# Where the squares in front of the up projection and of the embedding gate are added: GpSimd in place of VectorE and TensorE

## The chip, the cores and the metric

The kernel runs on one core of one Trainium2 chip. The metric is the device time of one execution in microseconds (us), the median of several runs. The engines are TensorE (PE in the rows; PEld is its weight load), VectorE (DVE), ScalarE (ACT), GpSimd (POOL) and SyncE (SP), which issues DMAs.

## The reference, cut to what matters

One step of a two-layer decoder over 512 prompt tokens and 8 sample tokens, together T = 520 tokens of D = 1024 features. Layer 0 mixes tokens with an mLSTM, layer 1 with sliding-window attention. Around the mixer every layer does the same:

```python
h = h + rmsnorm(mixer(rmsnorm(h, g_pre_mix)), g_post_mix)
h = h + rmsnorm(conv_ffn(rmsnorm(h, g_pre_ffn)), g_post_ffn)   # d_ff = 2816, causal conv of width 3
h = h + sigmoid(rmsnorm(h, g_ple) @ w_gate) * (p[i] @ w_proj)  # per-layer embedding
# rmsnorm(x, g) = x * rsqrt(mean(x * x) + eps) * g
```

The case is about two of these norms: the one in front of the ConvFFN (`g_pre_ffn`, stage `up`) and the one in front of the embedding gate (`g_ple`, stage `ple`). Each needs the sum of h squared over the 1024 features of every token.

## The kernel before, in words

Activations lie feature-major: 128 features on the partitions, KT = 8 tiles of features, the 520 tokens along the free dimension, in two halves q = 0 and q = 1 of HT = 260 tokens. Every weight tile and every activation tile is split into a high and a low part (`wH`, `wL`, `xH`, `xL`), and a product is three matmuls (`product`, `half_product`, L1173 to L1189): high by high, low by high, high by low. ScalarE makes the high parts, VectorE the low parts (`low`, L1827; `x_low`, L1851). Weight chunks come in by DMA into a ring of slots, issued by SyncE in the order of the stages. All order is written out by hand: each engine has its own program, and engines wait for each other on counting semaphores.

Around the change a layer goes like this, once after the mixer (stages `mout` or `sout`, then `up`) and once after the down projection (`down`, `pw`, then `ple`):

- PE ends the product y for half 0, then for half 1. VectorE sums the squares of y into `acc` (`add_unit`, L1897), PE sums `acc` over the partitions with a matmul by ones (`y_sum`, L1240), ScalarE takes the root (`root`, L763), VectorE the reciprocal (`one_over`, L1835).
- VectorE then runs through the `residual` steps (L1858), eight tiles k for each half q: y times gain times 1/rms into `cv` (L1865), h plus that (L1870), and the low part of the next input (L1853). All three read two operands from SBUF. ScalarE follows tile by tile with `inputs` (L780): the high part `xH`, and the square of h into `square(stage, q, k)`, a 128x260 tile.
- PE starts the next stage on half 0 alone (`first_half`, L1482, three chunks), then catches up on half 1 as its tiles come (`second_half`, L1494), then takes whole chunks (`chunk`, L1194). A chunk may start once the PSUM bank that it takes has been read (`free_after`, L1207): whole chunk 3 needs the read of chunk 0, chunk 5 that of chunk 3.
- The sum over the features of the squares is made in between. For q = 0 of `up` VectorE folds the eight tiles into one (`fold_squares`, L1843), and PE sums it over the partitions by one 128x128 matmul with ones (`square_sum`, L1231). For the three others of a layer (`GROUPED`, L108: `up` q = 1, `ple` q = 0, `ple` q = 1) PE adds: `square_group` (L1220) sends four tiles at a time through four 32-column groups of the array, ScalarE copies the result back (`group_sums`, L775), and `square_sum` makes the total of it. ScalarE takes the root (`pre_root`, L769) and VectorE the reciprocal (`pre_one_over`, L1839), by which the PSUM reads of the stage scale (`first_read`, `second_read`, `scaled_read`).

GpSimd works early (stretch before 190 us), and at the start of layer 1; in the stretches around the change it has only a small memset, and DMAs to issue.

Of the kernel before, what the change touches and what calls it, by code (L numbers as in the profile page):

```python
# [8 lines left out]
ALU = mybir.AluOpType  # L9
ACT = mybir.ActivationFunctionType  # L10
# [4 lines left out]
D = 1024  # L15
KT = D // P
SEQ, DEC = 512, 8
T = SEQ + DEC
HT = T // 2
# [85 lines left out]
ROOT = {("kv", 0): 1, ("mout", 0): 2, ("mout", 1): 3, ("down0", 0): 4, ("down0", 1): 5, ("qkv", 0): 6,  # L105
        ("sout", 0): 7, ("sout", 1): 8, ("down1", 0): 9, ("down1", 1): 10}
PREROOT = {(s, q): 2 * i + q + 1 for i, s in enumerate(("up0", "ple0", "up1", "ple1")) for q in range(2)}
GROUPED = {sq: n + 1 for n, sq in enumerate(sq for sq in PREROOT if sq[0][:2] != "up" or sq[1])}  # L108
POST = {"up0": "mout", "ple0": "down0", "up1": "sout", "ple1": "down1"}
G_PRE_MIX, G_POST_MIX, G_PRE_FFN, G_POST_FFN, G_PLE = range(5)  # L110

# [26 lines left out]
def build(nc, g):  # L138
    with ExitStack() as ctx:
# [19 lines left out]
        def sem(name):  # L159
            return ctx.enter_context(nc.semaphore(name))  # L160
# [26 lines left out]
        sq = sb("sq", [P, 2, T])  # L187
# [142 lines left out]
                                                          sem("gate_weights_ready"), sem("gate_parts_read"),  # L330
                                                          sem("gate_rows"), sem("gate_rows_read"))
        s_part, s_sqadd = sem("gate_parts_done"), sem("squares_added")
        s_psum, s_psumr = sem("pre_squares_by_group"), sem("pre_squares_by_group_read")
        s_fold = sem("pre_squares_added")
        s_raw0 = [sem(f"first_weights_in{c}") for c in range(2)]
        s_high0, s_low0 = sem("first_weights_high"), sem("first_weights_low")
        s_mm, s_read = sem("chunk_done"), sem("tile_read")
# [86 lines left out]
        def square(stage, q, k):  # L424

            if stage[:2] == "up":
                return squares_up[int(stage[2])][:, KT * q + k, :]
            if q == 0 and k < KT // 2:
                return sg[k // 2][:, tokens(k % 2)]
            return squares_ple[:, KT * q + k - KT // 2, :]  # L430
# [190 lines left out]
        def _(pool):  # L621
# [78 lines left out]
            pool.wait_ge(s_out, 16 * stored)  # L700
            pool.wait_ge(s_cps, 16)

            for layer in range(NL):
                up, down, ple = f"up{layer}", f"down{layer}", f"ple{layer}"

                if layer:
                    pool.wait_ge(s_hid, FT)
                    pool.wait_ge(s_out, 16 * stored)
                    pool.dma_start(convw[:], g.convw[layer]).then_inc(s_cw, 16)
                    pool.dma_start(prev[:], g.conv_prev[layer]).then_inc(s_cw, 16)  # L710

                pool.wait_ge(s_afin if layer == 0 else s_rope, NH + 1 if layer == 0 else 2 + KT)
                nc.gpsimd.memset(u[:, :, 0:2], 0.0).then_inc(s_pad, 1)
                if layer == 0:
                    for i, (r0, r1) in enumerate(COPIES):
                        pool.wait_ge(s_mm, CHUNK0["up0"] + 4 * i + 4)
                        pool.dma_start(g.v_s[r0:r1], g.vc_in[r0 + 1:r1 + 1]).then_inc(s_out, 16)
                    pool.wait_ge(s_mm, CHUNK0["up0"] + 4 * len(COPIES) + 4)
                    pool.dma_start(g.conv_old, g.conv_prev[:, :, :, 1, :]).then_inc(s_out, 16)
                    stored += len(COPIES) + 1  # L720
                pool.wait_ge(s_hid, FT * (layer + 1))
                pool.dma_start(g.newrows[layer], newrows[:]).then_inc(s_out, 16)
                stored += 1

                pool.dma_start(pin[:], g.p[layer]).then_inc(s_p, 16)
                if layer == 0:
                    pool.wait_ge(s_mm, CHUNK0["ple0"] + 1 + NEXTRA)
                    nc.gpsimd.memset(qpad[:], 0.0).then_inc(s_qz, 1)
                    for dst, src in ((sinks[:], g.sinks), (cos_t[:], g.cos_t), (sin_t[:], g.sin_t)):
                        pool.dma_start(dst, src).then_inc(s_swc, 16)  # L730
                    band_and_sinks(pool)
                    pool.wait_ge(s_qp, 1)
                    pool.dma_start(g.k_p, qk[:, 0:2, SEQ - WINDOW:SEQ]).then_inc(s_out, 16)
                    pool.dma_start(g.v_p, vs[:, :, SEQ - WINDOW:SEQ]).then_inc(s_out, 16)
                    pool.dma_start(g.k_s, kc[:, :, :, 1:WINDOW + 1]).then_inc(s_out, 16)
                    pool.wait_ge(s_vtr, 3)
                    pool.dma_start(g.v_s[WINDOW - 1], vnew[:]).then_inc(s_out, 16)
                    last_rotation(pool)
                    pool.wait_ge(s_ss, SUM["qkv", 0])
                    nc.gpsimd.memset(acc[:], 0.0).then_inc(s_acc, 1)  # L740
                    pool.wait_ge(s_rope, 2 + KT)
                    nc.gpsimd.memset(spad, 0.0).then_inc(s_spz, 1)
                    stored += 4
                    assert stored == STORED_L0
# [3 lines left out]
        def _(act):  # L748
# [20 lines left out]
            def pre_root(stage, q):  # L769

                act.wait_ge(s_squ, KT + PREROOT[stage, q])
                nc.scalar.activation(rstd[:, tokens(q)], sums[:, q, 0:HT], ACT.Sqrt, bias=eps[:, 0:1],
                                     scale=1.0 / (32 * D if (stage, q) in GROUPED else D)).then_inc(s_rootp, 1)

            def group_sums(stage, q):  # L775

                act.wait_ge(s_psum, GROUPED[stage, q])
                nc.scalar.activation(square(stage, q, 0), sums[:, q, 0:HT], ACT.Copy).then_inc(s_psumr, 1)

            def inputs(stage, k, q, layer, norm):  # L780

# [134 lines left out]
            def feed_forward(layer, mixer, y, beside):  # L916
# [33 lines left out]
                for k in range(KT):  # L950
                    inputs(up, k, 1, layer, G_PRE_FFN)
                    if k == 2:
                        high(up, 3)
                group_sums(up, 1)
                pre_root(up, 1)
                high(up, 4)
                high(up, 5)
# [68 lines left out]
                p_copy(5)  # L1026
                high(ple, 1)
                ple_input(0, 1)
                group_sums(ple, 0)
                p_copy(6)  # L1030
                high(ple, 2)
                ple_input(1, 1)
# [4 lines left out]
                for k in range(4, KT):  # L1037
                    ple_input(k, 1)
                high(ple, 3)
                group_sums(ple, 1)  # L1040
                high(ple, 4)
                pre_root(ple, 1)
                for c in range(5, KT):
# [128 lines left out]
        def _(pe):  # L1172
# [44 lines left out]
                elif r + k0 >= 2:  # L1217
                    pe.wait_ge(s_read, r + k0 - 1)

            def square_group(stage, q, part):  # L1220

                pe.wait_ge(s_sq, SQ0[stage] + KT * q + 4 * part + 4)
                if part == 0:
                    pe.wait_ge(s_root, ROOT[POST[stage], q])
                for j in range(4):
                    mm = nc.tensor.matmul(sums[32 * j:32 * j + 32, q, 0:HT], ones[:, 0:32], square(stage, q, 4 * part + j),  # L1226
                                          start=(part == 0), stop=(part == 1), skip_group_check=True)
                if part:
                    mm.then_inc(s_psum, 1)

            def square_sum(stage, q):  # L1231

                if (stage, q) in GROUPED:
                    pe.wait_ge(s_psumr, GROUPED[stage, q])
                else:
                    pe.wait_ge(s_root, ROOT[POST[stage], q])
                    pe.wait_ge(s_fold, int(stage[2]) + 1)
                nc.tensor.matmul(sums[:, q, 0:HT], ones, square(stage, q, 0), start=True, stop=True).then_inc(s_squ, 1)

            def y_sum(stage, q):  # L1240
# [272 lines left out]
            def feed_forward(layer, mixer, beside):  # L1513
# [15 lines left out]
                for k in range(4):  # L1529
                    for c in range(SPLIT):  # L1530
                        second_half(up, c, k, k + 1)
                square_group(up, 1, 0)
                square_group(up, 1, 1)
                for c in range(2):
                    second_half(up, c, 4, 5)
                square_sum(up, 1)
# [41 lines left out]
                for j in range(KT):  # L1578
                    c, jj = CHUNK0[pw] + j // 4, j % 4
                    if jj == 0:  # L1580
                        weights_ready(c)
                    for q in range(2):
                        if j >= 2:
                            pe.wait_ge(s_pwr, 2 * KT * layer + 2 * (j - 2) + q + 1)
                        for k in range(EKT):
                            mm = half_product(c, EKT * jj + k, (pH, pL), k, q, p_bank(j)[:, q, 0:HT], k == 0, k == EKT - 1)
                        mm.then_inc(s_mm if jj == 3 and q == 1 else s_pw, 1)
                    if j == 0:
                        y_sum(down, 1)
                    if j == 5:  # L1590
                        square_group(ple, 0, 0)
                        square_group(ple, 0, 1)

                yd = YREAD0[down]
                square_sum(ple, 0)
# [3 lines left out]
                for k in range(3):  # L1599
                    for c in range(SPLIT):  # L1600
                        second_half(ple, c, k, k + 1)
                square_group(ple, 1, 0)
                square_group(ple, 1, 1)
                for c in range(SPLIT):
                    second_half(ple, c, 3, 4)
                square_sum(ple, 1)
# [217 lines left out]
        def _(dve):  # L1824
# [14 lines left out]
            def pre_one_over(stage, q):  # L1839
                dve.wait_ge(s_rootp, PREROOT[stage, q])  # L1840
                chain.link(nc.vector.reciprocal(rstd[:, tokens(q)], rstd[:, tokens(q)]))

            def fold_squares(stage, q):  # L1843

                dve.wait_ge(s_sq, SQ0[stage] + KT * q + KT)
                tiles = squares_up[int(stage[2])][:, KT * q:KT * q + KT, :]
                for n in (4, 2):
                    chain.link(nc.vector.tensor_tensor(tiles[:, 0:n, :], tiles[:, 0:n, :], tiles[:, n:2 * n, :], ALU.add))
                nc.vector.tensor_tensor(tiles[:, 0, :], tiles[:, 0, :], tiles[:, 1, :], ALU.add).then_inc(s_fold, 1)

            def x_low(stage, k, q, layer, norm):  # L1851
                dve.wait_ge(s_xh, XSET[stage] + KT * q + k + 1)
# [347 lines left out]
            def feed_forward(layer, mixer, y, beside):  # L2200
# [35 lines left out]
                low(up, 2)  # L2236
                add_unit(mixer, 5, 1)
                add_unit(mixer, 6, 1)
                fold_squares(up, 0)

                dve.wait_ge(s_pad, layer + 1)
                one_over(mixer, 1, cg[:, tokens(1)])
# [524 lines left out]
```

## Time and profile before

| | |
|---|---|
| Median of 3 runs | 1296.57 us (1296.37 to 1296.8) |
| Span of the profiled execution | 1294.8 us, granted TensorE clock 1.000 |
| Busy: PE, DVE, ACT, POOL | 1287.4, 891.1, 594.0, 75.0 us |
| `square_group`, L1226 | 96 records of PE, 380 to 408 ns each, four at a time |
| VectorE's fold, L1848 and L1849 | 6 instructions |
| `group_sums`, L778 | 6 copies of ScalarE |

Only the span of the profiled execution is given, not its time as the runs count it; the median of the runs lies 1.8 us above the span. Times in the rows are from the span's start. A start is when an engine took the instruction up; an instruction that is blocked after that shows a longer duration. Instructions of VectorE and ScalarE overlap by some 0.08 us, so that starts, not durations, give the pace. The ends of PE's records are modelled, and there too the starts give the pace.

### The profile page before, as it was taken

Reading aid. Unit: us, or ns where it says so; the run is one execution under the profiler, and the core shown is the slowest. Engines: PE = TensorE matmul, PEld = TensorE weight load, DVE = VectorE, ACT = ScalarE, POOL = GpSimd, SP = SyncE. Lnnn points to the kernel's source line nnn. Section 1 sums busy time; section 2 is a strip of 40 time slices with the busy share of each in tenths; the row PEclk is TensorE's granted clock in tenths of the full one; section 3 lists DMA queues with packets and bytes.
Section 4 is the critical chain, followed back from the end, with each engine's and each line's share of the span. In section 5 each row is a group of like instructions: output and inputs, shape, how many; then the busy total and the mean of one; then the engine's idle time right before and its main releaser. Section 6 shows DMA issues by size and latency. Waiting matters only on the chain.

```text
span 1294.8 us, 25277 instructions
## 1 busy us (share of the span) xinstructions
PE 1287.4 (99%) x10786; PEld 1254.7 (97%) x10786; DVE 891.1 (69%) x1602; ACT 594.0 (46%) x1060; POOL 75.0 (6%) x117
## 2 busy tenths in 40 slices
PE   9999999999999999999999999999999999999998
PEld 8999989999999999999999978999999999999998
DVE  7899776987777774223897787688777777422385
ACT  6214565544444443223855677554444444222381
POOL 1112230000100000000031020000000000000000
PEclk9999999999999999999999999999999999999999
DMA  5435521213343233222314232311322323322231
GB/s 199 155 100 194 198 99 53 103 58 106 95 105 94 87 111 114 90 90 78 138 59 148 68 97 81 113 52 50 98 94 87 98 84 110 114 90 90 79 130 67
DMA packets 35616, 131.84 MB, mean 102 GB/s; under 512 B 4516, under 2 KB 5260, under 8 KB 35184
## 3 DMA queue, kind: packets, MB, share of 16 engines
q1 hardware_dynamic: 29664, 111.33, 26.8%
q0 software_dynamic: 5408, 18.26, 4.3%
q8 instruction: 85, 1.39, 0.4%
q10 hardware_dynamic: 432, 0.64, 0.2%
q14 instruction: 27, 0.22, 0.1%
HBM read 121.26 MB, written 10.08 MB: 101 GB/s over the span
## 4 chain that ended last, share of the span: by engine, by line
PE 95%; DVE 3%; ACT 1%; DMA 0%; issue 0%; ACTq 0%; DVEq 0%
PE tile L1177 24%; PE tile L1181 24%; PE tile L1179 24%; PE tile L1187 5%; PE tile L1188 5%; PE tile L1189 4%; PE tile L1649 1%; PE side L1187 1%; PE side L1188 1%; PE side L1189 1%; PE sums L1226 0%; DMA raw<-in_w_kv 0%; PE sums L1700 0%; PE sums L1348 0%; PE sums L1707 0%
## 5 line engine op out<-in xcount | busy, mean ns | idle before, releaser
L756 ACT ACTIVATE wH<-raw 128x1024 fp32r<-128x1024 f32 (+1 forms) x190 | 210.9, 1113 | 377.4 <-DMA raw<-in_w_up 145.9
L1177 PE MATMUL tile<-xH,wH 128*128 128x260 f32 x1798 | 362.7, 283 | 0.1
L1181 PE MATMUL tile<-xH,wL 128*128 128x260 f32 x1798 | 362.4, 283 | 0.0
L1179 PE MATMUL tile<-xL,wH 128*128 128x260 f32 x1798 | 361.8, 283 | 0.0
L1832 DVE TENSOR_TENSOR wL<-raw,wH 128x1024 fp32r<-128x1024 f32 (+1 forms) x190 | 245.7, 1294 | 154.5 <-ACT wH L756 150.4
L1177 PEld LDWEIGHTS tile<-xH,wH 128*128 128x128 f32 x1798 | 277.1, 188 | 3.5 <-issue 3.0
L1181 PEld LDWEIGHTS tile<-xH,wL 128*128 128x128 f32 x1798 | 277.2, 188 | 0.0
L1179 PEld LDWEIGHTS tile<-xL,wH 128*128 128x128 f32 x1798 | 276.4, 188 | 0.0
L1880 DVE SCALAR_TENSOR_TENSOR u<-tile,rstd 128x520 f32<-128x520 f32 x96 | 67.2, 700 | 119.5 <-PE tile L1181 119.4
L1177 PE MATMUL tile<-hidH,wH 128*128 128x260 f32 x616 | 124.3, 283 | 0.0
L1181 PE MATMUL tile<-hidH,wL 128*128 128x260 f32 x616 | 123.8, 282 | 0.0
L1179 PE MATMUL tile<-hidL,wH 128*128 128x260 f32 x616 | 123.8, 282 | 0.0
L1187 PE MATMUL tile<-xH,wH 128*128 128x260 f32 x400 | 116.0, 290 | 0.1
L1188 PE MATMUL tile<-xL,wH 128*128 128x260 f32 x400 | 113.1, 283 | 0.0
L1189 PE MATMUL tile<-xH,wL 128*128 128x260 f32 x400 | 112.8, 282 | 0.0
L1179 PEld LDWEIGHTS tile<-hidL,wH 128*128 128x128 f32 x616 | 95.1, 188 | 0.0
L1181 PEld LDWEIGHTS tile<-hidH,wL 128*128 128x128 f32 x616 | 94.9, 188 | 0.0
L1177 PEld LDWEIGHTS tile<-hidH,wH 128*128 128x128 f32 x616 | 94.8, 188 | 0.0
L1187 PEld LDWEIGHTS tile<-xH,wH 128*128 128x128 f32 x400 | 75.3, 188 | 2.8 <-issue 2.3
L1188 PEld LDWEIGHTS tile<-xL,wH 128*128 128x128 f32 x400 | 75.3, 188 | 0.3
L1189 PEld LDWEIGHTS tile<-xH,wL 128*128 128x128 f32 x400 | 75.3, 188 | 0.0
L977 ACT ACTIVATE cv<-u,taps 128x520 f32<-128x520 f32 x44 | 36.2, 824 | 48.2 <-DVE u L1880 47.8
(446 smaller groups left out, 1913.9 us busy)
## 6 DMA issues: line engine op xcount, KB each, us to landing
raw<-in_w_up SPq DMA_DIRECT2D x88, 512.0 KB, 3.6
raw<-in_w_down SPq DMA_DIRECT2D x32, 704.0 KB, 4.1
raw<-in_w_ple SPq DMA_DIRECT2D x16, 512.0 KB, 5.6
raw<-in_w_qo SPq DMA_DIRECT2D x12, 512.0 KB, 3.6
raw<-in_w_qkv SPq DMA_DIRECT2D x12, 512.0 KB, 3.5
raw<-in_w_kv SPq DMA_DIRECT2D x10, 512.0 KB, 3.7
cring<-in_c_in POOLq DMA_DIRECT2D x8, 512.0 KB, 4.8
out_c_s<-cring POOLq DMA_DIRECT2D x8, 512.0 KB, 3.2
```

The costliest lines, as they stand in the source:

```text
L756: nc.scalar.activation(wH[j][:, 0:n], raw[j][:, 0:n], ACT.Copy).then_inc(s_high, 1)
L977: nc.scalar.activation(dst[:], u[:, r, 2:], ACT.Identity, bias=taps[:, r, 3:4], scale=taps[:, r, 2:3]).then_inc(s_ca, 1)
L1177: nc.tensor.matmul(out[:, q, 0:HT], wh, x[0][:, k, tokens(q)], start=first, stop=False)
L1179: nc.tensor.matmul(out[:, q, 0:HT], wh, x[1][:, k, tokens(q)], start=False, stop=False)
L1181: mm = nc.tensor.matmul(out[:, q, 0:HT], wl, x[0][:, k, tokens(q)], start=False, stop=last)
L1187: nc.tensor.matmul(out, wh, x[0][:, k, tokens(q)], start=first, stop=False)
L1188: nc.tensor.matmul(out, wh, x[1][:, k, tokens(q)], start=False, stop=False)
L1189: return nc.tensor.matmul(out, wl, x[0][:, k, tokens(q)], start=False, stop=last)
L1649: nc.tensor.matmul(banks[half][:, e, at0 + 2 * HD - HD * m + k0:at0 + 3 * HD], queries[r, gp, m * P:m * P + P], qk[r, gp // 2, k0:HD * m + ...
L1832: nc.vector.tensor_tensor(wL[j][:, 0:n], raw[j][:, 0:n], wH[j][:, 0:n].bitcast(F32), ALU.subtract).then_inc(s_low, 1)
L1880: nc.vector.scalar_tensor_tensor(out=halves(dst), in0=bank(stage, c)[0:rows, :, 0:HT], scalar=scale, in1=halves(rstd[0:rows, :]), op0=ALU. ...
```

## The change

GpSimd gets a `fold_squares` of its own, and runs it four times in a layer: for `up` q = 0 and q = 1 behind the memset of `u`, and for `ple` q = 0 and q = 1 behind the load of `pin`. Each is a chain of seven adds of 128x260 tiles in place, total += square k for k = 1 to 7; an add waits for its square and for the add before it. VectorE's fold, PE's `square_group` and ScalarE's `group_sums` go. `square_sum` waits for GpSimd's last add, and stands where it stood.

```diff
-GROUPED = {sq: n + 1 for n, sq in enumerate(sq for sq in PREROOT if sq[0][:2] != "up" or sq[1])}
+FOLDED = {sq: n + 1 for n, sq in enumerate(PREROOT)}
...
+            folds = Chain(pool, s_folds)
+
+            def fold_squares(stage, q):
+
+                total = square(stage, q, 0)
+                pool.wait_ge(s_sq, SQ0[stage] + KT * q + 2)
+                for k in range(1, KT):
+                    if k > 1:
+                        pool.wait_ge(s_sq, SQ0[stage] + KT * q + k + 1)
+                    step = nc.gpsimd.tensor_tensor(total, total, square(stage, q, k), ALU.add)
+                    if k < KT - 1:
+                        folds.link(step)
+                step.then_inc(s_pooled, 1)
...
                 nc.gpsimd.memset(u[:, :, 0:2], 0.0).then_inc(s_pad, 1)
+                for q in range(2):
+                    fold_squares(up, q)
...
                 pool.dma_start(pin[:], g.p[layer]).then_inc(s_p, 16)
+                for q in range(2):
+                    fold_squares(ple, q)
...
-                                     scale=1.0 / (32 * D if (stage, q) in GROUPED else D)).then_inc(s_rootp, 1)
-
-            def group_sums(stage, q):
-
-                act.wait_ge(s_psum, GROUPED[stage, q])
-                nc.scalar.activation(square(stage, q, 0), sums[:, q, 0:HT], ACT.Copy).then_inc(s_psumr, 1)
+                                     scale=1.0 / D).then_inc(s_rootp, 1)
...
-                if (stage, q) in GROUPED:
-                    pe.wait_ge(s_psumr, GROUPED[stage, q])
-                else:
-                    pe.wait_ge(s_root, ROOT[POST[stage], q])
-                    pe.wait_ge(s_fold, int(stage[2]) + 1)
+                pe.wait_ge(s_root, ROOT[POST[stage], q])
+                pe.wait_ge(s_pooled, FOLDED[stage, q])
...
-                square_group(up, 1, 0)
-                square_group(up, 1, 1)
                 for c in range(2):
                     second_half(up, c, 4, 5)
                 square_sum(up, 1)
...
-                    if j == 5:
-                        square_group(ple, 0, 0)
-                        square_group(ple, 0, 1)
...
-                square_group(ple, 1, 0)
-                square_group(ple, 1, 1)
                 for c in range(SPLIT):
                     second_half(ple, c, 3, 4)
                 square_sum(ple, 1)
...
-                fold_squares(up, 0)
```

The order of GpSimd's instructions at the start of layer 0's `up`, before:

```order
L618 TENSOR_TENSOR xL<-kvq,xH 128x520 x2
L713 MEMSET u 128x2x2
L717 DMA out_v_s<-in_vc_in 16x4096 x3
L717 DMA out_v_s<-in_vc_in 16x3968
L719 DMA out_conv_old<-in_conv_prev 11264x8
L722 DMA out_newrows<-newrows 128x440
L725 DMA pin<-in_p 128x1040
```

and in the change, up to the next instruction that was there before:

```order
L617 TENSOR_TENSOR xL<-kvq,xH 128x520 x2
L726 MEMSET u 128x2x2
L711 TENSOR_TENSOR squares_up_101<-squares_up_101 128x260 x14
L732 DMA out_v_s<-in_vc_in 16x4096 x3
L732 DMA out_v_s<-in_vc_in 16x3968
L734 DMA out_conv_old<-in_conv_prev 11264x8
L737 DMA out_newrows<-newrows 128x440
L740 DMA pin<-in_p 128x1040
L711 TENSOR_TENSOR u<-u 128x260 x3
L711 TENSOR_TENSOR u<-u,squares_ple 128x260 x4
L711 TENSOR_TENSOR squares_ple<-squares_ple 128x260 x7
L745 MEMSET qpad 128x656
```

Fourteen adds come in ahead of the copies of the value cache (`out_v_s`), and fourteen between the load of `pin` and the memset of `qpad`; layer 1 has the same, with nothing behind its last fourteen.

The order of PE's instructions around the sum for `up` q = 1, layer 0, before (`tile` and `side` are PSUM banks, `wH_52` and the like the ring's slots):

```order
L1189 MATMUL side<-xH,wL_59 128x260
L1226 MATMUL sums<-squares_up_101,const 32x260 [waits root_ready,squared]
L1226 MATMUL sums<-squares_up_101,const 32x260 x3
L1226 MATMUL sums<-squares_up_101,const 32x260 [waits squared]
L1226 MATMUL sums<-squares_up_101,const 32x260 x3
L1187 MATMUL tile<-xH,wH_52 128x260 [waits x_ready]
L1188 MATMUL tile<-xL,wH_52 128x260
L1189 MATMUL tile<-xH,wL_53 128x260
L1187 MATMUL tile<-xH,wH_55 128x260
L1188 MATMUL tile<-xL,wH_55 128x260
L1189 MATMUL tile<-xH,wL_56 128x260
L1238 MATMUL sums<-squares_up_101,const 128x260 [waits pre_squares_by_group_read]
```

and in the change:

```order
L1198 MATMUL side<-xH,wL_59 128x260
L1196 MATMUL tile<-xH,wH_52 128x260 [waits x_ready]
L1197 MATMUL tile<-xL,wH_52 128x260
L1198 MATMUL tile<-xH,wL_53 128x260
L1196 MATMUL tile<-xH,wH_55 128x260
L1197 MATMUL tile<-xL,wH_55 128x260
L1198 MATMUL tile<-xH,wL_56 128x260
L1233 MATMUL sums<-squares_up_101,const 128x260 [waits pre_squares_added_by_pool,root_ready]
```

The eight matmuls by 32 columns are gone, and the one by 128 columns waits for GpSimd in place of ScalarE's copy.

## Rows read from the trace of the kernel before

**Rows 1.** The page's first part: busy us (share of the span) xinstructions.

```profile
PE 1287.4 (99%) x10786; PEld 1254.7 (97%) x10786; DVE 891.1 (69%) x1602; ACT 594.0 (46%) x1060; POOL 75.0 (6%) x117
```

**Rows 2.** Chain that ended last, layer 1's `up`: start us, us, engine, tile, line.

```profile
846.84 1.79 DVE cg L1837
...
875.75 0.61 DVE u L1880
876.41 0.51 PE tile L1177 x2
```

**Rows 3.** Timeline of PE, layer 0's `up`: start us, us, engine, instruction, count.

```profile
231.20 0.60 PE L1249 MATMUL sums<-acc,const 128*128 128x260 f32 x2
...
261.98 0.40 PE L1181 MATMUL tile<-xH,wL 128*128 128x260 f32 x2
262.42 0.50 PE L1177 MATMUL tile<-xH,wH 128*128 128x260 f32 x2
```

**Rows 4.** Timeline of DVE, the same stretch; in brackets idle before, and its releaser.

```profile
218.35 0.49 DVE L1853 SCALAR_TENSOR_TENSOR xL<-h,front,xH 128x260 fp32r<-128x260 f32 x1 [1.10 <-ACT xH L783]
...
228.19 0.96 DVE L1901 TENSOR_TENSOR acc<-acc,sq 128x260 f32<-128x260 f32 x2
...
232.85 1.78 DVE L1837 RECIPROCAL cg<-cg 128x260 f32<-128x260 f32 x1 [1.36 <-ACT cg L766]
...
244.25 1.77 DVE L1841 RECIPROCAL rstd<-rstd 128x260 f32<-128x260 f32 x1
...
261.67 0.69 DVE L1880 SCALAR_TENSOR_TENSOR u<-tile,rstd 128x520 f32<-128x520 f32 x1
```

**Rows 5.** Timeline of PE, layer 0's `ple`, around the group for q = 1.

```profile
640.64 0.28 PE L1188 MATMUL side<-xL,wH 128*128 128x260 f32 x1
640.76 0.28 PE L1189 MATMUL side<-xH,wL 128*128 128x260 f32 x1
640.97 1.08 PE L1226 MATMUL sums<-squares_ple,const 128*32 128x260 f32 x16
...
643.17 0.60 PE L1238 MATMUL sums<-squares_ple,const 128*128 128x260 f32 x2
...
647.91 0.41 PE L1177 MATMUL tile<-xH,wH 128*128 128x260 f32 x2
```

**Rows 6.** Timeline of DVE, layer 0's `ple`.

```profile
617.22 0.49 DVE L1853 SCALAR_TENSOR_TENSOR xL<-h,front,xH 128x260 fp32r<-128x260 f32 x1 [0.51 <-ACT xH L783]
...
618.85 0.49 DVE L1853 SCALAR_TENSOR_TENSOR xL<-h,front,xH 128x260 fp32r<-128x260 f32 x1 [0.40 <-ACT xH L783]
...
623.24 0.49 DVE L1853 SCALAR_TENSOR_TENSOR xL<-h,front,xH 128x260 fp32r<-128x260 f32 x1 [0.75 <-ACT xH L783]
...
638.40 1.77 DVE L1841 RECIPROCAL rstd<-rstd 128x260 f32<-128x260 f32 x1
...
644.32 1.78 DVE L1841 RECIPROCAL rstd<-rstd 128x260 f32<-128x260 f32 x1 [2.22 <-ACT rstd L772]
646.13 0.43 DVE L1893 TENSOR_TENSOR u<-tile,rstd 128x260 f32<-128x260 f32 x1
```

**Rows 7.** View of one line: duration ns min/median/max, first and last start us, forms.

```profile
L611 POOL TENSOR_TENSOR prob<-prob,kvq x4: 997/1010/1032, 134.3 to 173.1; 128x384 f32<-128x384 f32 x4
...
L614 DVE TENSOR_TENSOR cg<-const,sq x2: 691/1007/1323, 114.8 to 136.0; 128x512 f32<-128x512 f32 x2
...
L573 POOL CAST bandB<-const x2: 1042/1391/1740, 692.2 to 693.9; 128x1024 bf16<-128x1024 f32 x2
```

**Rows 8.** Timeline of POOL, before 190 us and at 674 us.

```profile
114.51 1.06 POOL L607 TENSOR_TENSOR ktok<-ktok,wcol 128x512 f32<-128x512 f32 x1
...
177.95 5.10 POOL L618 TENSOR_TENSOR xL<-kvq,xH 128x520 fp32r<-128x520 f32 x4 [3.89 <-ACT xH L892]
...
672.76 1.29 POOL L565 TENSOR_SCALAR partsB<-partsB,sinks 128x8 bf16<-128x8 bf16 x1
674.14 0.85 POOL L565 TENSOR_SCALAR partsB<-partsB,sinks 128x8 bf16<-128x8 bf16 x1
```

More of the change, by code:

```diff
@@ L332, in build @@
         s_part, s_sqadd = sem("gate_parts_done"), sem("squares_added")
-        s_psum, s_psumr = sem("pre_squares_by_group"), sem("pre_squares_by_group_read")
-        s_fold = sem("pre_squares_added")
+        s_pooled, s_folds = sem("pre_squares_added_by_pool"), sem("pool_fold_steps")
         s_raw0 = [sem(f"first_weights_in{c}") for c in range(2)]
@@ L953, in feed_forward @@
                         high(up, 3)
-                group_sums(up, 1)
                 pre_root(up, 1)
@@ L1028, in feed_forward @@
                 ple_input(0, 1)
-                group_sums(ple, 0)
                 p_copy(6)
@@ L1039, in feed_forward @@
                 high(ple, 3)
-                group_sums(ple, 1)
                 high(ple, 4)
@@ L1218, in free_after @@
                     pe.wait_ge(s_read, r + k0 - 1)
-            def square_group(stage, q, part):
-                pe.wait_ge(s_sq, SQ0[stage] + KT * q + 4 * part + 4)
-                if part == 0:
-                    pe.wait_ge(s_root, ROOT[POST[stage], q])
[L1225 to L1229, printed above, removed]
-            def square_sum(stage, q):
-                if (stage, q) in GROUPED:
-                    pe.wait_ge(s_psumr, GROUPED[stage, q])
-                else:
-                    pe.wait_ge(s_root, ROOT[POST[stage], q])
-                    pe.wait_ge(s_fold, int(stage[2]) + 1)
+            def square_sum(stage, q):
+                pe.wait_ge(s_root, ROOT[POST[stage], q])
+                pe.wait_ge(s_pooled, FOLDED[stage, q])
                 nc.tensor.matmul(sums[:, q, 0:HT], ones, square(stage, q, 0), start=True, stop=True).then_inc(s_squ, 1)
@@ L1841, in pre_one_over @@
                 chain.link(nc.vector.reciprocal(rstd[:, tokens(q)], rstd[:, tokens(q)]))
[L1843 to L1849, printed above, removed]
             def x_low(stage, k, q, layer, norm):
```

## The prediction

> **What bounds the kernel now.** I read the page's first part first: PE is busy for 1287.4 of 1294.8 us [rows 1], at a granted clock of 1.000, so only two things can move the time: work taken off PE, and waits put into it. The change takes work off PE, but off a stretch in which PE may have no use for it. So the chain of waits comes next, around the places of the four sums. In layer 1's `up` it leaves PE: it goes from the reciprocal of the post-norm root (846.84) through VectorE and ends on VectorE's read of chunk 3, L1880, behind which PE goes on at 876.41 [rows 2]. The timelines say how close it is. In layer 0 PE's matmuls of a whole chunk come 0.24 us apart, but between 261.98 and 262.42 lie 0.44 us [rows 3]: chunk 5 waited 0.2 us for the read of chunk 3, which ends at 261.67 + 0.69 = 262.36 [rows 4]. From 232.85 to there VectorE never waits for PE. So in `up` two engines bind together: what PE saves there it waits for at chunk 5, and what VectorE loses there the kernel loses.
>
> In `ple` it is otherwise. The second reciprocal of VectorE (644.32) had waited 2.22 us for ScalarE's root, which waits for PE's sum, so VectorE was free at 642.10 [rows 6]; and PE starts chunk 3 at 647.91 [rows 5], 1.35 us after the read of chunk 0, which frees its bank, ended at 646.13 + 0.43 = 646.56 [rows 6]. There PE leads, and its saving counts.
>
> **The change part by part.** *PE, `square_group` gone.* Matmuls of a half chunk come 0.12 us apart (640.64, 640.76). From 640.76 to the sum at 643.17 lie ten such steps, 1.20 us, if the group weren't there; it takes 2.41 [rows 5]. So a group costs PE 1.21 us. Of the three in a layer the one in `up` is worth 0 (chunk 5 waits instead), the two in `ple` up to 2.42.
>
> *ScalarE, six copies gone; VectorE, its fold gone.* Worth nothing. The root waits for PE's sum in any case, and VectorE's fold lay in front of the reciprocal at 232.85, before which VectorE stood idle for another 1.36 us, for the root behind PE's `y_sum` [rows 4].
>
> *GpSimd, 56 adds of 128x260.* No add of this size is in the trace. Four plain adds of two 128x520 tiles took 5.10 us [rows 8], 1.275 each; half the elements give 0.64. From this and the 384-element row, 1.010 [rows 7], a straight line gives 0.77; the 512-element row, 1.06 with one operand broadcast [rows 8], gives 0.54. I take 0.64, from the row of the same form. GpSimd has nothing else to do there, the DMAs queued behind the adds wait for later PE chunks anyway, and a tile of squares comes every 1.1 us or so; by itself it would keep up, and the last sum would be there in time.
>
> *What the adds do to VectorE.* This is the term that decides. VectorE's instruction of L614 takes 0.69 us alone, and 1.32 at 114.8 [rows 7], where GpSimd's add of 114.51 runs until 115.57 [rows 8]. It ended at 116.13, so its own 0.69 began at about 115.44: it stood still until 0.13 us before GpSimd's add ended. The other way round GpSimd's cast, 1.04 alone, took 1.74 behind a VectorE instruction [rows 7]. So the two take turns, an instruction at a time, when both read two tiles of SBUF; and the residual steps, L1865, L1870 and L1853, all read two. One add then costs a fully loaded VectorE between 0.51 (0.64 less 0.13) and 0.64; I take 0.60. The ends are 0.41 (0.54 less 0.13) and 0.77.
>
> The sum, for one layer. `up`, half 0: seven adds, 4.20, of which the wait of 1.10 for ScalarE covers as much [rows 4]. The rest, 3.10, puts off the last `add_unit`, which ended at 228.19 + 0.96 = 229.15 and is needed by PE's `y_sum` at 231.20 [rows 3, 4]: 2.05 us of slack, 1.05 late. `up`, half 1: VectorE goes without a pause from the reciprocal on; the seventh add falls into the reciprocal at 244.25, which reads one tile; six cost 3.60. Chunk 5 is late by 4.65.
>
> `ple`, half 0: the seventh add again falls into a reciprocal, six cost 3.60, and the waits for ScalarE, 0.51 + 0.40 + 0.75 = 1.66, take as much of it back [rows 6]: 1.94. Half 1: the sixth add falls mostly into the last wait for `xH`, five cost 3.00. VectorE reaches 638.40 later by 4.94, is free at 642.10 + 4.94 = 647.04, its reciprocal starts 2.72 later than now, and the read of chunk 0 ends at 649.28 in place of 646.56. Chunk 3 can't start at 647.91: PE loses 1.4, and what it saved with the two groups goes into that wait. Together 4.65 + 1.4 = 6.05 a layer, 12.1 in both. Against the span 1294.8 this gives 1306.9; the same on the median, 1296.57, gives **1308.7 us**.
>
> With 0.41 an add, `up` loses 2.46 (half 0 stays within its slack); in `ple` VectorE is late by 2.46 - 1.66 + 2.05 = 2.85 at 638.40, its read of chunk 0 ends at 647.19, and chunk 3 starts 0.7 earlier than now: 1.76 a layer, 1300.1. With 0.77: 2.24 + 4.62 in `up`, and 6.81 late in `ple`, 3.3 at chunk 3: 10.1 a layer, 1316.8.
>
> By the Trainium skill (GPSIMD Engine Reference, Performance versus the Vector engine) a GpSimd add of 2048 fp32 elements takes 4497 ns. An estimate for 260 of them is 0.57 us against the 0.64 of the row; it would make the forecast about 1305.
>
> **The rivals.** *VectorE keeps GpSimd out.* VectorE's instructions overlap, so GpSimd may get no turn until VectorE pauses. For it: an eight-element operation of GpSimd took 1.29 us and another 0.85 [rows 8]. Against it: such a thing is over as soon as VectorE ends one or two instructions of 0.7, so turns were had. Then VectorE loses nothing in the residual steps, but the seven adds of half 1 start at 244.25 and end, with 4.5 us of their own and 1.1 of a low part of weights between, at 249.9. The reciprocal for half 1 would start 3.1 us later than now, and chunk 5 with it; in `ple` the same count from 638.40 gives 644.0 in place of PE's sum at 643.17, 0.8 late. That is 3.9 a layer, 1304.4. The Trainium skill (SBUF — State Buffer, Who interferes with whom) says that whichever instruction starts first keeps the shared port pair to its end; that fits either order, and the rows show both.
>
> *The other side: the adds cost VectorE nearly nothing.* Mechanism: an add finds its turn in the short gaps between dependent residual steps, or holds the port only while it reads its 260 elements. Then `up` stays as it is (chunk 5 waits for VectorE), and in `ple` VectorE's second reciprocal can start at 642.10, PE keeps its 2.42: 4.8 in both layers, 1291.8. It decides below about 0.30 us an add: there the six adds in `up` cost 1.8 a layer, and `ple` gives 1.9. For it: the adds are short, and no row shows one of this size against these steps. Against it: the 0.69 that became 1.32.
>
> *In between*, at 0.25 to 0.35 us an add, loss and gain cancel to within 2 us by the same sum: 1294.8 to 1298.1.
>
> **How the numbers follow.** Turns, as in the sum: 0.70, and 1308.7 with it. GpSimd kept out: 0.16, 1304.4. In between: 0.06. Nearly no cost: 0.08, 1291.8. A measurement here tells 0.2%, 2.6 us, from no change. Turns and the kept-out case lie above that: slower 0.86. Same 0.06, faster 0.08. The range goes from 1300, the foot of the sum, to 1315, a little inside its top, and leaves out the two cheap cases.
>
> **What would show it.** In the changed profile: L1865, L1870 and L1853 of half 1 come up to 0.6 us later each time an add lies in front, so that the eight residual steps of `up` take 15 us in place of 11.4 between the two reciprocals; PE's busy time falls a little while its idle time rises by some 12 us, in waits for `xL`, for the sum of half 1 and for the reads of chunks 0 and 3; GpSimd's adds take 0.6 to 1.1 us, a wait for VectorE among it. If GpSimd is kept out, the steps keep their 11.4 us and the adds bunch behind 244.25 and 638.40. If the steps keep their pace and the adds lie beside them, the price of an add is wrong, and the time falls.

## The result, and the profile after

The changed kernel takes 1302.99 us (median of 4 runs, 1302.91 to 1303.19) against 1296.53 before: ratio 1.0049, 95% interval 1.0037 to 1.0061, 6.46 us slower. Direction and range were right; the 12.1 us of the forecast were nearly twice too many. The profiled execution took 1302.91 us, its span is 1301.1. In the kernel with GpSimd's adds for half 1 of `up` alone, one execution of five took 1773.98 us at a granted clock of 0.654; its time below is the median of the other four (1301.85 to 1302.32), and its trace, which is of the slow one, is not used.

The page's first part and the head of its fourth, the chain that ended last:

```profile
PE 1287.0 (99%) x10690; PEld 1255.8 (97%) x10690; DVE 908.4 (70%) x1596; ACT 592.7 (46%) x1054; POOL 127.4 (10%) x173
...
PE 86%; DVE 11%; ACT 2%; issue 1%; DMA 0%; POOL 0%; ACTq 0%; DVEq 0%; POOLq 0%
```

Against [rows 1] VectorE is busy 17.3 us longer, although its fold is gone: time in which it is held counts as busy. GpSimd, whose busy time grew by 52 us, has 0% of the chain; VectorE's share of it is 11% where it was 3% before.

PE's waits point elsewhere (what waited, for what: us in total, times, longest):

```profile
PE sums L1233 <- POOL squares_up L711: 4.4, 2, 2.2
...
PE side L1196 <- ACT pwo L1014: 1.0, 2, 0.5
```

By this list the loss would be PE's wait for GpSimd's last add in `up`, which the prediction had not foreseen. Whether it is, the experiments decide.

To see where the time went, each stage is measured from PE's `y_sum` for half 0, once before and once after. The anchors of before that are not shown yet, PE and VectorE:

```profile
208.88 0.60 PE L1249 MATMUL sums<-acc,const 128*128 128x260 f32 x2
608.23 0.60 PE L1249 MATMUL sums<-acc,const 128*128 128x260 f32 x2
609.38 1.78 DVE L1837 RECIPROCAL cg<-cg 128x260 f32<-128x260 f32 x1 [1.63 <-ACT cg L766]
623.65 1.77 DVE L1837 RECIPROCAL cg<-cg 128x260 f32<-128x260 f32 x1
```

Timeline of PE after, layer 0's `up` (anchor, second `y_sum`, sum of half 1, chunk 5) and `ple` (anchor, a product of `pw`, sum of half 1, chunk 3):

```profile
208.76 0.60 PE L1244 MATMUL sums<-acc,const 128*128 128x260 f32 x2
...
231.78 0.71 PE L1244 MATMUL sums<-acc,const 128*128 128x260 f32 x2 [0.54 <-DVE acc L1881]
...
248.50 1.21 PE L1233 MATMUL sums<-squares_up,const 128*128 128x260 f32 x2 [2.21 <-POOL squares_up L711]
...
265.85 0.51 PE L1186 MATMUL tile<-xH,wH 128*128 128x260 f32 x2
...
611.67 0.60 PE L1244 MATMUL sums<-acc,const 128*128 128x260 f32 x2
...
628.75 0.39 PE L1196 MATMUL side<-pH,wH 128*128 128x260 f32 x1 [0.51 <-ACT pwo L1014]
...
645.85 0.68 PE L1233 MATMUL sums<-squares_ple,const 128*128 128x260 f32 x2
...
650.92 0.51 PE L1186 MATMUL tile<-xH,wH 128*128 128x260 f32 x2
```

From anchor to chunk 5 `up` takes 57.09 us, before 53.54 (to 262.42, [rows 3]): 3.55 lost. From anchor to chunk 3 `ple` takes 39.25, before 39.68 (to 647.91, [rows 5]): 0.43 gained. Layer 1 gives +3.54 and -0.46 in the same way; together 6.20 of the 6.3 us between the spans. So `up` lost everything, and `ple` gained a little.

Timeline of VectorE after, `up` of layer 0:

```profile
230.78 0.95 DVE L1881 TENSOR_TENSOR acc<-acc,sq 128x260 f32<-128x260 f32 x2
233.54 1.78 DVE L1825 RECIPROCAL cg<-cg 128x260 f32<-128x260 f32 x1 [1.82 <-ACT cg L783]
...
237.36 0.48 DVE L1833 SCALAR_TENSOR_TENSOR xL<-h,front,xH 128x260 fp32r<-128x260 f32 x1
...
238.50 0.98 DVE L1833 SCALAR_TENSOR_TENSOR xL<-h,front,xH 128x260 fp32r<-128x260 f32 x1
...
239.81 0.97 DVE L1850 TENSOR_TENSOR h<-h,cv 128x260 f32<-128x260 f32 x1
...
247.69 1.76 DVE L1829 RECIPROCAL rstd<-rstd 128x260 f32<-128x260 f32 x1
...
251.30 1.77 DVE L1829 RECIPROCAL rstd<-rstd 128x260 f32<-128x260 f32 x1
...
265.10 0.69 DVE L1860 SCALAR_TENSOR_TENSOR u<-tile,rstd 128x520 f32<-128x520 f32 x1
```

and GpSimd's adds there:

```profile
224.46 1.64 POOL L711 TENSOR_TENSOR squares_up<-squares_up 128x260 f32<-128x260 f32 x1 [0.39 <-ACT squares_up L797]
...
238.38 0.82 POOL L711 TENSOR_TENSOR squares_up<-squares_up 128x260 f32<-128x260 f32 x1 [8.61 <-ACT squares_up L797]
239.59 0.90 POOL L711 TENSOR_TENSOR squares_up<-squares_up 128x260 f32<-128x260 f32 x1 [0.39 <-ACT squares_up L797]
...
247.49 0.87 POOL L711 TENSOR_TENSOR squares_up<-squares_up 128x260 f32<-128x260 f32 x1 [0.41 <-ACT squares_up L797]
```

PE's chunk 5 (265.85) follows VectorE's read of chunk 3 (265.10 + 0.69), as it did before. From the first reciprocal of the sums (247.69) to that read VectorE takes 17.41 us, before 17.42 (244.25 to 261.67, [rows 4]): nothing is lost there, though PE's late sum lies in it. So the question is what makes VectorE late by 247.69. The add of 238.38 lies under the L1833 of 238.50, which takes 0.98 us where the one before took 0.48; the add of 239.59 lies under the L1850 of 239.81, 0.97 in place of 0.42. Five instructions between the two reciprocals are stretched like this, three on L1833 by 0.50 us and two on L1850 by 0.55, and the stretch takes 14.15 us (233.54 to 247.69) in place of 11.40 (232.85 to 244.25, [rows 4]). The seventh add, at 247.49, falls into the reciprocal, which keeps its 1.76. The add of 224.46 shows the other order: it took 1.64 us behind a VectorE instruction of 1.21.

VectorE in `ple` after:

```profile
612.82 1.78 DVE L1825 RECIPROCAL cg<-cg 128x260 f32<-128x260 f32 x1 [1.63 <-ACT cg L783]
...
621.42 0.87 DVE L1845 SCALAR_TENSOR_TENSOR cv<-y_down,front,cg 128x260 f32<-128x260 f32 x1
...
627.61 1.77 DVE L1825 RECIPROCAL cg<-cg 128x260 f32<-128x260 f32 x1
...
645.02 1.77 DVE L1829 RECIPROCAL rstd<-rstd 128x260 f32<-128x260 f32 x1
...
648.63 1.77 DVE L1829 RECIPROCAL rstd<-rstd 128x260 f32<-128x260 f32 x1
650.44 0.89 DVE L1873 TENSOR_TENSOR u<-tile,rstd 128x260 f32<-128x260 f32 x2
```

Half 0 takes 14.79 us (before 14.27), half 1 17.41 (before 14.75, to 638.40 in [rows 6]); the second reciprocal no longer waits.

### The profile page after: what moved, and what is told of

Its sections match the earlier page's. It is cut to its first block, busy times and chain, and to the rows that moved or that the text cites. A ratio compares the mean times of both kernels' runs of the same rounds, so it can differ in the third digit from the quotient of the medians.

```text
span 1301.1 us, 25177 instructions
## 1 busy us (share of the span) xinstructions
PE 1287.0 (99%) x10690; PEld 1255.8 (97%) x10690; DVE 908.4 (70%) x1596; ACT 592.7 (46%) x1054; POOL 127.4 (10%) x173
## 4 chain that ended last, share of the span: by engine, by line
PE 86%; DVE 11%; ACT 2%; issue 1%; DMA 0%; POOL 0%; ACTq 0%; DVEq 0%; POOLq 0%
PE tile L1186 24%; PE tile L1190 24%; PE tile L1188 24%; PE tile L1196 2%; PE tile L1197 2%; PE tile L1198 2%; DVE cv L1845 2%; DVE xL L1833 2%; DVE h L1850 2%; DVE wL L1820 1%; DVE cg L1825 1%; PE tile L1637 1%; DVE rstd L1829 1%; DMA raw<-in_w_kv 0%; PE sums L1688 0%
## 5 line engine op out<-in xcount | busy, mean ns | idle before, releaser
L1820 DVE TENSOR_TENSOR wL<-raw,wH 128x1024 fp32r<-128x1024 f32 (+1 forms) x190 | 248.4, 1308 | 152.7 <-ACT wH L773 148.6
```

Source lines behind the costliest of these rows:

```text
L1820: nc.vector.tensor_tensor(wL[j][:, 0:n], raw[j][:, 0:n], wH[j][:, 0:n].bitcast(F32), ALU.subtract).then_inc(s_low, 1)
```

## The experiments

The theory after this reading: an add of GpSimd that reads SBUF holds up the two-operand instruction of VectorE behind it by some 0.50 us, and VectorE is what `up` waits for. The main rival: the late sum, PE's 2.21 us at 248.50. The medians of before that ran beside the experiments are 1296.48 to 1296.56 us.

**One stage at a time.** The folds are put on GpSimd for the members of one set, the others stay on PE's groups or VectorE. The set is `(("up", 0), ("up", 1))` in the first kernel, `(("ple", 0), ("ple", 1))` in the second:

```diff
-GROUPED = {sq: n + 1 for n, sq in enumerate(sq for sq in PREROOT if sq[0][:2] != "up" or sq[1])}
+POOLED = (("up", 0), ("up", 1))
+FOLDED = {sq: n + 1 for n, sq in enumerate(sq for sq in PREROOT if (sq[0][:-1], sq[1]) in POOLED)}
+GROUPED = {sq: n + 1 for n, sq in enumerate(sq for sq in PREROOT if sq not in FOLDED and (sq[0][:2] != "up" or sq[1]))}
```

> GpSimd adds the squares of both halves of up; in ple PE's groups stay as they were before the change. Theory (turns: an add of GpSimd makes VectorE's two-operand step behind it wait 0.50 us, and up carries the whole loss): chunk 5 of up comes 3.4 to 3.5 us later in each layer, as in the changed kernel, and the stretch of ple is as it was before; 1296.5 + 2 x 3.5 = 1303.5 us, a little above the changed kernel. Rival (the loss is spread over all four sums, 1.6 us a half layer): about 1299.7 us.

> GpSimd adds the squares of both halves of ple; in up VectorE's fold and PE's group stay as before. Theory: in ple VectorE is 3.2 us late at the end of half 1, but it had 2.2 us to spare there, and PE saves 2.4 us of groups and gives most of it back in waits; the changed kernel leaves ple 0.4 us earlier in each layer than it entered it, measured against before. So 1296.5 - 0.8 = 1295.7 us. Rival (the loss is spread over all four sums): about 1299.7 us.

Measured: `up` alone 1303.97 us, ratio 1.0058 (1.0045 to 1.0070); `ple` alone 1296.16, ratio 0.9997 (0.9988 to 1.0006). The whole loss is in `up`; `ple` is worth nothing that can be told. The two differences, +7.45 and -0.36, add up to 7.1 against the 6.5 of both together, nearer than the intervals can tell.

**Adds that nobody waits for.** GpSimd's seven adds for half 1 of `up` beside the kernel before, into a tile that is dead by then; only ScalarE's first high part of the hidden tile behind `up` has a wait for the last of them:

```diff
+            def idle_adds(up, layer):
+                total = square(up, 0, KT - 1)
...
+                    step = nc.gpsimd.tensor_tensor(total, total, square(up, 1, k), ALU.add)
```

> The kernel before, with the seven adds of GpSimd for half 1 of up laid beside it, behind the same squares; their result is used by nobody, PE sums with its group as before. Theory (turns): VectorE's steps of half 1 take 14.1 us between the two reciprocals in place of 11.4, chunk 5 comes 2.7 us later in each layer, 1296.5 + 5.5 = 1302 us, although no engine waits for GpSimd's sum. Rival (late sum: the loss in up is PE's wait of 2.2 us for GpSimd's last add): nobody waits for the sum here, so 1296.5 us, and the steps may even be slow without cost.

Measured: 1302.18 us, ratio 1.0043 (1.0030 to 1.0056). VectorE between the two reciprocals:

```profile
232.98 1.78 DVE L1856 RECIPROCAL cg<-cg 128x260 f32<-128x260 f32 x1 [1.36 <-ACT cg L783]
...
247.13 1.76 DVE L1860 RECIPROCAL rstd<-rstd 128x260 f32<-128x260 f32 x1
```

14.15 us, to the hundredth what the changed kernel has, with a sum that comes from PE. The last add ends at 247.80, and ScalarE's instruction with the wait starts at 260.98, behind VectorE. The loss needs no wait for GpSimd.

**The same adds, and PE waits for them.** The set is `(("up", 1),)`.

> GpSimd adds the squares of half 1 of up alone, and PE's sum waits for it; half 0 of up and all of ple are as before. It differs from the kernel with idle adds by the wait for the sum, and from the kernel with both halves of up by half 0. Theory (the loss is VectorE's, PE's wait of 2.2 us for the last add lies in front of a wait that comes anyway): the same as with idle adds, 1302.2 us, and 1.8 us below both halves of up (1304.0), which is what half 0 costs. Rival (the wait for the sum costs as well): 1303.5 to 1304 us, and half 0 would be free.

Measured: 1302.10 us, ratio 1.0043 (1.0029 to 1.0056), the same as with idle adds. PE's longest wait of the changed kernel costs nothing: it stands in front of chunk 5, which waits for VectorE in any case. It is a near thing there: PE's matmul before chunk 5 starts at 265.36 in the changed kernel and the pace is 0.24 us, so that PE had 0.25 us to spare. The difference to both halves of `up`, 1.87 us or 0.9 a layer, is what half 0 costs by the medians; the intervals of the two ratios overlap, but in the changed kernel's trace half 0 comes to 0.8 a layer as well.

**Writes alone.**

```diff
-                    step = nc.gpsimd.tensor_tensor(total, total, square(stage, q, k), ALU.add)
+                    step = nc.gpsimd.memset(total, 1.0)
```

> The changed kernel with each add replaced by a memset of the same 128x260 tile, behind the same waits and in the same chains: GpSimd writes as much as before and reads nothing; the sums of squares are left out. Theory (what VectorE and GpSimd share is the reading of SBUF): VectorE's steps of half 1 of up are back at 11.4 us between the reciprocals, up loses nothing, ple gains 1.0 to 1.8 us a layer from the groups that PE no longer has: 1293 to 1294.5 us. The Trainium skill (SBUF — State Buffer, Who interferes with whom) says that a VectorE instruction with two SBUF inputs is held up by a GpSimd instruction that reads SBUF, not by one that only writes it; the theory's number is this rule's. Rival (any GpSimd instruction that touches SBUF holds VectorE up, or its semaphores do): 1301 to 1303 us, with the steps at 13 to 14 us.

Measured: 1293.25 us, ratio 0.9975 (0.9965 to 0.9985). The view of the line (ns, min/median/max) and VectorE's reciprocals:

```profile
L711 POOL MEMSET squares_up<- x28: 314/316/317, 215.4 to 856.3; 128x260 f32 x28
```

```profile
232.68 1.78 DVE L1825 RECIPROCAL cg<-cg 128x260 f32<-128x260 f32 x1 [3.71 <-ACT cg L783]
...
244.06 1.77 DVE L1829 RECIPROCAL rstd<-rstd 128x260 f32<-128x260 f32 x1
```

and PE's `y_sum` for half 0 and its chunk 5:

```profile
208.70 0.60 PE L1244 MATMUL sums<-acc,const 128*128 128x260 f32 x2
...
262.23 0.51 PE L1186 MATMUL tile<-xH,wH 128*128 128x260 f32 x2 [0.40 <-DVE u L1860]
```

11.38 us between the reciprocals, and 53.53 from anchor to chunk 5 (before 53.54): with the same number of GpSimd instructions, waits and signals, and the same DMAs queued behind them, VectorE isn't held at all, nor is GpSimd. By the Trainium skill (SBUF — State Buffer, Who interferes with whom) a GpSimd instruction that only writes doesn't contend with a VectorE instruction of two SBUF inputs; this run agrees. It also shows what the work taken off the other engines is worth with nothing set against it: 3.27 us in both layers, and by the anchors none of it in `up`.

**One tile read in place of two.**

```diff
-                    step = nc.gpsimd.tensor_tensor(total, total, square(stage, q, k), ALU.add)
+                    step = nc.gpsimd.tensor_scalar(total, square(stage, q, k), 1.0, None, ALU.add)
```

> The changed kernel with each add replaced by square k plus the constant 1 into the same place, behind the same waits and in the same chains: GpSimd reads one tile in place of two; the sums of squares are left out. Theory (what is shared is the reading of SBUF, and it is held as long as GpSimd reads): half the reading, so some 0.25 us for each instruction that stands in front of VectorE in place of 0.50; up loses 1.3 us a layer and more or less gives back what ple gains: 1296 to 1298 us, the steps of half 1 at 12.5 to 13 us. Rival A (only an operation with two inputs takes the shared port): as with the memset, 1293.3 us, steps 11.4 us. Rival B (the hold doesn't depend on what is read): 1302 to 1303 us, steps 14 us.

Measured: 1294.64 us, ratio 0.9986 (0.9977 to 0.9994), below what the theory gave. The line of GpSimd here, and in the changed kernel:

```profile
L711 POOL TENSOR_SCALAR squares_up<-squares_up x28: 860/1036/1898, 215.4 to 858.0; 128x260 f32<-128x260 f32 x28
```

```profile
L711 POOL TENSOR_TENSOR squares_up<-squares_up x28: 738/847/1647, 215.5 to 864.7; 128x260 f32<-128x260 f32 x28
```

VectorE here:

```profile
232.67 1.78 DVE L1825 RECIPROCAL cg<-cg 128x260 f32<-128x260 f32 x1 [2.87 <-ACT cg L783]
...
237.64 0.62 DVE L1833 SCALAR_TENSOR_TENSOR xL<-h,front,xH 128x260 fp32r<-128x260 f32 x1
...
244.79 1.77 DVE L1829 RECIPROCAL rstd<-rstd 128x260 f32<-128x260 f32 x1
```

VectorE is held, but by 0.14 us a hit (0.62 in place of 0.48), the stretch takes 12.12 us. GpSimd's instruction itself is longer than the add (1036 ns against 847 in the median), so its length is not what VectorE waits for. Both rivals fall; so does the simple share of half, and why it is 0.14 and not 0.25 stays open.

**Half the columns.** The idle adds on 130 of the 260 columns.

```diff
-step = nc.gpsimd.tensor_tensor(total, total, square(up, 1, k), ALU.add)
+step = nc.gpsimd.tensor_tensor(total[:, 0:HT // 2], total[:, 0:HT // 2], square(up, 1, k)[:, 0:HT // 2], ALU.add)
```

> The kernel with idle adds, each add on 130 columns in place of 260; the result is still used by nobody. Theory (the hold goes with the elements that are read): 0.25 us an add, steps 12.6 to 12.9 us between the reciprocals of half 1, 1296.5 + 2 x 1.3 = 1299.2 us. Rival (a fixed price for each instruction, from its start and its signal): 14.1 us, 1302.2 us as with the whole tiles.

Measured: 1298.74 us, ratio 1.0017 (1.0008 to 1.0026).

```profile
232.96 1.78 DVE L1856 RECIPROCAL cg<-cg 128x260 f32<-128x260 f32 x1 [1.36 <-ACT cg L783]
...
237.92 0.70 DVE L1872 SCALAR_TENSOR_TENSOR xL<-h,front,xH 128x260 fp32r<-128x260 f32 x1
...
245.37 1.77 DVE L1860 RECIPROCAL rstd<-rstd 128x260 f32<-128x260 f32 x1
```

0.22 us a hit, 12.41 us for the stretch, a little below what the theory gave: the price goes with the elements of the add, and there is no fixed part that one would see. But two half tiles are as much to read as the one whole tile of the run before, which held VectorE for 0.14: across operations the elements read do not give the price, and what does is not shown.

**One half of `ple` at a time.** The sets `(("ple", 1),)` and `(("ple", 0),)`.

> GpSimd adds the squares of half 1 of ple alone; all else as before. Theory: PE saves one group, 1.2 us a layer; VectorE is 2.7 us late at the end of half 1, of which 2.2 lie in its old wait for the root, so the read of chunk 0 ends 0.45 us later and chunk 3 of ple starts 0.8 us earlier in each layer, bound by that read: 1296.5 - 1.7 = 1294.8 us. Rival (PE's saving is used up, as with both halves of ple): 1296.2 us.

> GpSimd adds the squares of half 0 of ple alone; half 1 of ple is summed by PE's group, up is as before. Theory: PE saves one group, 1.2 us a layer, but comes to ScalarE's copies of pw 0.6 us too early and waits there; VectorE goes into half 1 some 0.5 us late, and its old wait of 2.2 us for the root takes that in. So 0.55 us a layer: 1296.5 - 1.1 = 1295.4 us. Rival (the 0.5 us of VectorE come through to chunk 3): 1296.0 to 1296.5 us.

Measured: half 1 alone 1295.31 us, ratio 0.9995 (0.9986 to 1.0004); half 0 alone 1296.58, ratio 1.0000 (0.9991 to 1.0009). Half 1 came out 0.5 us above its number and 0.9 below its rival's; it is the fastest version that still adds all the squares, but not to be told from before. Half 0 was a miss; its time is its rival's. PE and VectorE there:

```profile
625.47 0.39 PE L1212 MATMUL side<-pH,wH 128*128 128x260 f32 x1 [0.51 <-ACT pwo L1028]
...
631.97 0.39 PE L1212 MATMUL tile<-xH,wH 128*128 128x260 f32 x1
...
641.14 1.08 PE L1253 MATMUL sums<-squares_ple,const 128*32 128x260 f32 x16
...
644.49 1.78 DVE L1871 RECIPROCAL rstd<-rstd 128x260 f32<-128x260 f32 x1 [1.86 <-ACT rstd L795]
```

This kernel's anchor is 608.40. The group for half 1 starts 32.74 us behind it, as it does before (640.97 behind 608.23): the 1.21 us of the group are gone already. Half a microsecond went into the wait for ScalarE's copies of `pw`, with 0.15 beside it, and the rest into gaps such as the 0.34 us in front of 631.97 (0.12 without a wait), where chunk 1 starts; the low parts of its weights come from a VectorE that is late (0.5 us at its reciprocal of half 1). The group had been filling these waits. So VectorE's lateness reaches PE through the weights, and not through the read in front of chunk 3, as the rival had it: the second reciprocal still waits for the root, 1.86 us, and starts 36.09 us behind the anchor, as before.

## Why the prediction was right in direction and twice too large

- **Two engines bind in `up`, and PE's group is worth nothing there**: right. With writes alone `up` neither gains nor loses: chunk 5 comes 53.53 us behind the anchor, before 53.54.
- **ScalarE's copies and VectorE's fold at nothing**: right for `up`, by the same run; in `ple` no run parts the copies from the groups.
- **GpSimd and VectorE take turns when both read two tiles**: right, but the condition is too narrow. The memset excludes signals and writes, the idle adds exclude a late sum; and a GpSimd operation that reads one tile held VectorE too, for 0.14 us. The cast of [rows 7], from which the prediction took the other order, reads one tile as well.
- **"I take 0.60"** is the term that was mis-sized. The bracket for a loaded VectorE was 0.51 to 0.64, and the hits of half 1 of `up` measure 0.50 (0.98 less 0.48) and 0.55 (0.97 less 0.42), the foot of it. VectorE doesn't wait for the whole of an add as it is recorded: the one of 238.38 ends at 239.20, but VectorE's instruction, which ended at 239.48, must have begun its own 0.48 at about 239.00. The Trainium skill (SBUF — State Buffer, Summary: rules for kernel authors) has the second instruction blocked until the first finishes; that is near, but by this row it goes on 0.2 us earlier, as far as GpSimd's recorded end can be trusted.
- **"Six cost 3.60" in half 1 of `up`**: five hits, 2.6 together, and the rest from the sixth, which falls where VectorE had waited for `xH` before: 2.75. Half 0: forecast 1.05 late, measured 0.70 at `y_sum` (23.02 against 22.32 from the anchor) and 0.81 at VectorE's reciprocal. So 3.55 in place of 4.65 a layer.
- **Half 0 of `ple`, 3.60 less 1.66**: 0.52 late in place of 1.94. The waits took in most, and hits were cheaper, as the 0.39 of 621.42 (0.87 less 0.48). Half 1: 2.66 in place of 3.00. Together 3.18 in place of 4.94.
- **Chunk 3 waits for the read of chunk 0**: right as a mechanism (the read of 650.44 is what PE's 650.92 follows), but the reciprocal starts 0.87 us later than before, measured from the anchor, where 2.72 were forecast, and chunk 3 came 0.43 earlier in place of 1.4 later. At chunk 3 this makes 3.7 of the 5.6 us that the forecast had too many.
- **PE's saving in `ple`, up to 2.42 a layer**: an upper bound that nothing reaches. With writes alone it is 1.6 (half of 3.27); in the change PE's sum of half 1 comes 0.76 earlier.
- **"By itself it would keep up, and the last sum would be there in time"**: wrong for `up`. The held VectorE is 3.56 us late behind the last squares (38.93 us from the anchor to 247.69, before 35.37), and with them the last add; PE waits 2.21 us, without cost.
- **Rivals.** GpSimd kept out: the stretch would have kept 11.4 us; it took 14.15. Nearly no cost: the price is some 0.50, above the 0.30 at which it would have turned.

With 0.50 in the prediction's own sum, `up` gives 0.35 + 3.00 and `ple` 0.3 a layer, 7.3 in all and 1303.9 us; with 0.52, the mean of the five hits of half 1 of `up`, 8.2 and 1304.8. The price is most of the error; with 0.52 the 0.9 a layer that is left is half 0 of `ple`, 1.46 late by that sum and 0.52 as measured.

## What to carry to other kernels

An elementwise operation on GpSimd is not free because GpSimd is idle: where it reads SBUF beside a VectorE that is busy with two-operand instructions, price each one by what it takes from VectorE (here 0.50 to 0.55 us in `up` for two tiles of 128x260, 0.22 for half of them, 0.14 with one input, nothing for a write), and let it fall into reciprocals, which kept their 1.76 us, or into VectorE's waits. The longest wait in the list need not be the one that costs; adds that nobody waits for were as dear as adds that PE waits for. And a group of matmuls that is removed gives back less than its length where it had been filling waits behind it.

## What the runs showed of the hardware that was not expected

In the changed kernel PE's clock fell at the end of its wait for the last add. Windows (us, PE busy, PEld, DVE, ACT, POOL, granted clock of PE, DMA share, GB/s):

```profile
246.00:248.00 2.00, 0.29 (x3) 0.08 (x1) 2.00 (x5) 0.93 (x3) 1.34 (x2) 1.00 0.00 0
248.00:250.00 2.00, 1.50 (x5) 1.34 (x6) 1.97 (x3) 0.26 (x1) 0.36 (x1) 0.56 0.00 0
250.00:252.00 2.00, 2.00 (x12) 2.00 (x12) 2.00 (x3) 2.00 (x3) 0.00 (x0) 0.59 0.00 0
```

Behind 2.21 us without work the granted clock is near its lower level (1.2 GHz), and from 249.7 to 251.5 half chunks come 0.215 us apart in place of 0.12. But the wait alone does not do it. With the adds of `up` alone PE waits as long at the same place, and the clock stays at 1.00; the sum, chunk 5 and a window of that kernel:

```profile
248.44 0.68 PE L1268 MATMUL sums<-squares_up,const 128*128 128x260 f32 x2 [2.21 <-POOL squares_up L715]
...
265.79 0.51 PE L1202 MATMUL tile<-xH,wH 128*128 128x260 f32 x2 [0.39 <-DVE u L1910]
```

```profile
248.00:250.00 2.00, 1.55 (x11) 1.53 (x12) 1.97 (x3) 0.84 (x2) 0.30 (x1) 1.00 0.00 0
```

What sets the two apart is not shown. The lower clock cost nothing here: chunk 5 comes 57.05 us behind the anchor (208.74) in that kernel and 57.09 in the changed one.

And a hold of VectorE depends on what GpSimd reads, not on how long GpSimd's instruction is: the one-input operation, the longer of the two, held it for 0.14 us, the add for 0.50.
